# State steps of the second prompt tile inside the joint chunk stage, and one set of weight places for the first tile and the gathers

## The reference, cut to what matters

```python
    def step(S, inp):
        r_t, d_t, k_t, v_t, kk_t, a_t = inp
        Skk = jnp.einsum('bhvk,bhk->bhv', S, kk_t)
        S = (S * d_t[:, :, None, :]
             - Skk[..., None] * (kk_t * a_t)[:, :, None, :]
             + v_t[..., None] * k_t[:, :, None, :])
        y_t = jnp.einsum('bhvk,bhk->bhv', S, r_t)
        return S, y_t
...
    s1, i1 = lax.top_k(s[:, :, 0], PEER_TOPK)
    s2, i2 = lax.top_k(s[:, :, 1], PEER_TOPK)
    cand_s = (s1[..., :, None] + s2[..., None, :]).reshape(n, PEER_HEADS, PEER_TOPK * PEER_TOPK)
...
    top_s, top_pos = lax.top_k(cand_s, PEER_TOPK)
    eidx = jnp.take_along_axis(cand_i, top_pos, axis=-1)
    gate = jax.nn.softmax(top_s, axis=-1)
    u = expert_u[eidx].astype(F32)
    h = jax.nn.gelu(jnp.einsum('nhkd,nd->nhk', u, xr.astype(F32)), approximate=False)
    out = jnp.einsum('nhk,nhkd->nd', gate * h, expert_v[eidx].astype(F32))
```

## Time and profile before

| | us |
|---|---|
| median of 3 runs | 3025.03 |
| lowest, highest | 3024.61, 3034.01 |
| profiled execution | 3024.4 |
| its span | 3022.6 |

### The profile page before, as it was taken

One profiled execution on the slowest core, in us unless ns is written; L12 is line 12 of the kernel. 1 busy time (PEld: TensorE's weight loads), 2 busy tenths in 40 slices (PEclk: granted clock), 3 DMA queues, 4 the chain that ended last, 5 costly groups with the idle time before them and its releaser, 6 DMA issues. The chain is left out here.

```text
span 3022.6 us, 33166 instructions
## 1 busy us (share of the span) xinstructions
PE 2145.5 (71%) x11513; PEld 1128.9 (37%) x11513; DVE 1785.6 (59%) x4171; ACT 683.5 (23%) x1972; POOL 1064.2 (35%) x995
## 2 busy tenths in 40 slices
PE   7989896568776867685577676676857768555554
PEld 3447685325443533332225222243324435222221
DVE  3454438355885754764746847557745455955555
ACT  2222121112222211212511115221113322121111
POOL 1033122333664633333333434333342222354442
PEclk9999898779987978896789787887979879677788
DMA  4330430899989999999999999999999999899998
GB/s 156 104 140 1 163 126 1 307 388 390 409 314 396 387 411 416 373 395 409 358 393 418 404 417 400 358 419 419 388 417 418 419 382 420 306 364 420 420 420 331
DMA packets 152164, 1025.97 MB, mean 339 GB/s; under 512 B 17852, under 2 KB 19180, under 8 KB 34112
## 3 DMA queue, kind: packets, MB, share of 16 engines
q0 software_dynamic: 116416, 823.23, 67.2%
q1 hardware_dynamic: 35584, 200.62, 16.9%
HBM read 1003.34 MB, written 19.44 MB: 338 GB/s over the span
## 5 line engine op out<-in xcount | busy, mean ns | idle before, releaser
L1364 POOL DMA_INDIRECT fl_pairs<-in_peer_uv,fl_row_at x652 | 743.3, 1140 | 1206.4 <-PE fl_acc L1337 1085.4
L1337 PE MATMUL fl_acc<-fl_pairs,fl_diag 128*64 128x512 f32 x2608 | 835.9, 745 | 419.4 <-ACT fl_diag L1310 399.8
L1290 DVE CUSTOM_DVE_ANT_0 fl_pairs<-fl_pairs,fl_rows 128x1024 f32<-128x1024 f32 x652 | 790.2, 1233 | 430.7 <-DMA fl_pairs<-in_peer_uv,fl_row_at 430.0
L1337 PEld LDWEIGHTS fl_acc<-fl_pairs,fl_diag 128*64 128x64 f32 x2608 | 281.0, 161 | 821.2 <-issue 775.2
L1316 ACT ACTIVATE fl_acts<-fl_dots 128x2 f32<-128x2 f32 x384 | 78.1, 203 | 1253.4 <-DVE fl_dots L1290 1253.1
L1310 ACT ACTIVATE fl_diag<-constants_sb,fl_mix 128x64 f32<-128x64 f32 x768 | 224.4, 341 | 292.5 <-DVE fl_mix L1280 291.1
L1337 PE MATMUL fl_acc<-fl_more,fl_diag 128*64 128x512 f32 x464 | 149.5, 743 | 87.2 <-ACT fl_diag L1310 87.1
L1364 POOL DMA_INDIRECT fl_more<-in_peer_uv,fl_row_at x116 | 132.3, 1140 | 219.0 <-PE fl_acc L1337 198.9
L1290 DVE CUSTOM_DVE_ANT_0 fl_more<-fl_more,fl_rows 128x1024 f32<-128x1024 f32 x116 | 139.6, 1222 | 78.5 <-DMA fl_more<-in_peer_uv,fl_row_at 78.1
L1280 DVE TENSOR_TENSOR fl_mix<-fl_row_gate,fl_acts 128x2 f32<-128x2 f32 x384 | 74.7, 195 | 129.0 <-ACT fl_acts L1316 77.4
L1710 PE MATMUL aacc<-pc_piece,at_xT 128*128 128x512 f32 x288 | 138.9, 625 | 8.3 <-PEq L1623 8.3
(11 more groups left out here) (571 smaller groups left out, 2870.6 us busy)
## 6 DMA issues: line engine op xcount, KB each, us to landing
pc_piece<-in_kvq_by_pair SPq DMA_DIRECT2D x36, 1024.0 KB, 9.3
pc_piece<-in_query_by_head SPq DMA_DIRECT2D x32, 1024.0 KB, 9.6
pc_piece<-in_past_k SPq DMA_DIRECT2D x16, 1024.0 KB, 14.1
pc_piece<-in_past_v SPq DMA_DIRECT2D x16, 1024.0 KB, 12.4
ro_w_ring<-in_rwkv_w_rkv SPq DMA_DIRECT2D x24, 512.0 KB, 4.5
pc_piece<-in_out_by_pair SPq DMA_DIRECT2D x12, 1024.0 KB, 9.4
fl_pairs<-in_peer_uv,fl_row_at POOLq DMA_INDIRECT x652, 15.0
ft_ring<-in_query_by_head SPq DMA_DIRECT2D x8, 1024.0 KB, 5.0
```

Of the source, the lines that this page charges most:

```text
L1290: dve.tensor_tensor_reduce(pair, pair, self.rows[:, u % 2, j, :], 1.0, 0.0, ALU.mult, ALU.add, self.dots[:, u % 2, q, j:j + 1]).then_inc(* ...
L1337: mm = pe.matmul(self.acc[j * FOLD:(j + 1) * FOLD, half, :], self.diag[:, self.summed % self.DIAGS, j, :], self.pair(g)[:, D + half * HALF ...
L1364: pool.indirect_dma_start(self.pair(g), None, self.io["peer_uv"], bass.IndirectOffsetOnAxis(ap=self.row_at[:, u % TILES, j, q:q + 1], axis ...
```

## The change

Four parts:

1. In the joint stage a pair's state steps follow its group: one step per tick (PE `state_step`, L2457 of the changed kernel; VectorE `add_state`, L2601), beside the next pair's work; the last pair's eight steps stand at the stage's end. `half_outputs` of tile 1 has no steps left: 6 ticks in place of 13.
2. Four places (`early`) are there from the start. `FirstTile` uses them for its weights, its vectors, its gate and its turned rows; later they are four of the ring's eight places. The rows of tile 0 for the dots have a buffer of their own (`first_rows`), spread at tick 24 in the joint stage.
3. In the joint stage the query weights are used two to a tick (ticks 23 to 30), the choice is drawn together (ticks 27 to 48), the experts' table goes out at tick 52 and comes in at 54, and the first four gathers are issued at tick 55. The gates' table follows on its own.
4. For all six tiles the experts and the gates travel apart: out, in, out, in at four ticks that follow each other, each "in" waiting for its own write. Gathers wait for the experts alone. The turns to end with are 7, 9, 17, 18, 31 in place of 11, 12, 19, 20, 32; from 55 on they are as before.

```diff
@@ Flow @@
-        self.ring, self.rows = sb("pairs", [P, self.KEPT, 2 * D]), sb("rows", [P, 2, GROUPS, D])
+        self.ring, self.rows = sb("pairs", [P, self.KEPT - self.EARLY, 2 * D]), sb("rows", [P, GROUPS, D])
...
-        for u, out_at, in_at in self.turns:
-            if out_at == n:
-                self.turn_rows_out(pool, u)
-            if in_at == n:
-                self.turn_rows_in(pool, u)
+        for u, first in self.turns:
+            if first == n:
+                self.experts_out(pool, u)
+            if first + 1 == n:
+                self.experts_in(pool, u)
+            if first + 2 == n:
+                self.gates_out(pool, u)
+            if first + 3 == n:
+                self.gates_in(pool, u)
...
+    def first_gathers(self, pool):
+
+        pool.wait_ge(*self.expert_in.at(16 * GROUPS))
+        for g in range(self.EARLY):
+            self.gather(pool, g)
@@ half_chunks @@
+                def state_step(g, c):
+
+                    if not prompt or g < 0:
+                        return
+                    if c == 0:
+                        pe.wait_ge(*gp_done.at(g + 1))
+                        pe.wait_ge(*fp_done.at(g + 1))
...
+                    if g + c > 0:
+                        pe.wait_ge(*step_done.at(NCH * g + c))
+                    for r in range(2):
+                        mm = pe.matmul(bank[3][half(r), stepped(c)], x.Ft[half(r), c, g, :], x.G[half(r), c, g, :], tile_position=(r * N, r * N))
+                    mm.then_inc(*step_psum.by())
...
+                    dve.wait_ge(*step_psum.at(NCH * g + c + 1))
+                    dve.tensor_tensor(x.G[:, c + 1, g, :], bank[3][:, stepped(c)], x.G[:, c + 1, g, :], ALU.add).then_inc(*step_done.by())
@@ half_outputs @@
-    TICKS = NCH + 5
+    LEAD = NCH if x.sample else 1
+    TICKS = LEAD + 5
...
+                if not x.sample:
+                    sp.wait_ge(*flow.landed(5))
@@ FirstTile @@
-        if n == self.ticks:
-            self.flow.turn_rows_out(pool, 0)
-            self.flow.turn_rows_in(pool, 0)
+        if n == 24:
+            pool.wait_ge(*self.normed.at(1))
+            self.flow.spread_rows(pool, 0)
+        if n == self.KNOWN + 2:
+            self.flow.experts_out(pool, 0)
+        if n == self.KNOWN + 4:
+            self.flow.experts_in(pool, 0)
+        if n == self.KNOWN + 5:
+            pool.wait_ge(*self.queries.at(4))
+            self.flow.first_gathers(pool)
...
@@ program and experts_and_attention @@
-        half_outputs(core, io, flow, x, rows, 11, rows=((0, 1),))
+        half_outputs(core, io, flow, x, rows, 7)
...
-            second_tile(core, io, flow, x, rows, ops, [(12, {}), (19, {}), (20, {}), (32, {})])
+            second_tile(core, io, flow, x, rows, ops, [(9, {}), (17, {}), (18, {}), (31, {})])
...
-            (110, dict(choose=2, side=15)), (112, dict(side=15)), (125, dict(side=60, end=12, turn=((2, 14, 16),))), (131, {}), (132, {}),
+            (110, dict(choose=2, side=15)), (112, dict(side=15)), (125, dict(side=60, end=12, turn=((2, 13),))), (131, {}), (132, {}),
```

More of the change, by code:

```diff
@@ L2457, in _ @@
                     beside.tensor(pe, tick + 7)
+                    state_step(b - 1, 7)
+                for c in range(NCH):
+                    state_step(NG - 1, c)
             @block.scalar
@@ L2667, in _ @@
                     pe.wait_ge(*start_in.at(16))
-                for c in range(NCH):
-                    if c > 0 and not x.sample:
-                        pe.wait_ge(*step_done.at(c))
-                    elif c > 1:
+                for c in range(NCH if x.sample else 0):
+                    if c > 1:
                         pe.wait_ge(*step_done.at(c - 1))
@@ L2690, in _ @@
                 mm.then_inc(*y_tok.by())
[L2691 removed]
+                for n in range(LEAD + 3, TICKS + 1):
                     flow.tensor(pe, n)
@@ L2695, in _ @@
             def _(act):
-                for n in range(1, NCH + 3):
+                for n in range(1, LEAD + 3):
                     flow.scalar(act, n)
@@ L2709, in _ @@
                 flow.vector(dve, 1)
-                for c in range(NCH):
+                if not x.sample:
+                    flow.vector(dve, 2)
+                for c in range(NCH if x.sample else 0):
                     dve.wait_ge(*step_psum.at(c + 1))
@@ L2902, in vector_steps @@
             part = choice.best_of(dve, choice.scores, q)
-            for i in range(4):
-                advance(part, 6)
-                n += 1
-                if i < 3:
-                    yield n
+            advance(part, 10)
+            yield n + 1
             drain(part)
+            n += 2
         part = choice.rest(dve, 0)
-        while n < self.ticks:
+        while n < self.KNOWN:
             yield n
```

160 lines of the change are left out of this document (105 added, 55 removed).

## The result

| | before | after |
|---|---|---|
| median of 9 runs each, us | 3026.84 | 3043.39 |
| lowest to highest, us | 3024.06 to 3039.56 | 3034.07 to 3057.47 |
| the profiled execution (its span), us | 3024.4 (3022.6) | 3047.2 (3045.4) |

The ratio is 1.0049, with a 95% interval from 1.0034 to 1.0065: the changed kernel is about 15 us slower by the ratio, 16.6 by the medians.

The account below looks back on a forecast made before the run. The prediction took PE and VectorE to bound the start, then idle DMA time to decide. Its terms, +3 (DMA account), -2 (one turn more) and +5 (tables), sum to +6, giving 3030 us; own range 3018 to 3042, whole range 3006 to 3050.

Parts of the forecast that it names:

- Start of the outputs' stage: End of the joint stage: summed tick by tick, the next stage starts at 560 us (bounds 545 and 572), before 538.3.
- the state terms up to there: Joint stage, ticks 1 to 48: state steps add 1.7 at first, 3 on PE, 4.0 on VectorE, 3 for handing over.
- I add 3 for handing over: Joint stage, ticks 31 to 48: PE waits for VectorE in each tick with a state step, 3 us in all.
- GpSimd's wait for the gate table: End of the joint stage: the sum to 560 has no term of its own for this wait.
- The signs of the mechanism: Joint stage: VectorE above 90% busy from 457 to 520, PE waiting for `step_done`; DMA share near 0.9 for 50 us after.
- The DMA account: Behind the outputs' stage's start: the same bytes are through at 638 against 635, +3 us, with 9 us of holes.
- One turn more in the stage to 55: Stage to turn 55, 24 turns for 23: part of the added turn fills DMA holes, -2 us (bounds -5 and 0).
- The tables' way: Tables of tiles 2 and 3: two waits each, no gather behind the write, +5 us (bounds 0 and 20).
- Taking the state steps out of `half_outputs` gives nothing by itself: Outputs' stage of tile 1: 541 to 590 us was full of gathers, which covered the steps; gain 0.
- Free state steps: Faster rival, joint stage: steps fit in gaps, next stage starts at 545 to 548, 3011 us; chance 0.33.
- The double wait: Slower rival, tables of tiles 1 to 3: two waits empty the DMA queue, 23 us in place of 5, 3048; chance 0.22.
- Early gathers late: Rival, end of the joint stage: GpSimd reaches tick 55 late, four gathers start with the next stage, 3040; chance 0.07.

Follow-up runs that it names:

- e7: e5 with all state steps in the outputs' stage, as in the kernel before; 3001.05 us, ratio 0.9903.
- e5: The changed kernel with one wait for both tables of tiles 1 to 5, and tile 0's gate table awaited three ticks later; 3019.11 us, ratio 0.9971.
- e9: The changed kernel, but for tiles 2 and 3 each write and its wait stand two ticks apart, with gathers between; 3027.67 us, ratio 1.0005.
- e4: The changed kernel without the four gathers ahead of the joint stage's end; 3046.36 us, ratio 1.0058.
- e6: e5 with the state steps of pairs 4 to 7 moved to the outputs' stage; 3003.25 us, ratio 0.9914.

## Why the prediction was right or wrong

The forecast was 3030, 6 us over before. Measured were 3043.4, about 15 over: outside the forecast's own 3018 to 3042 and 5 under the slower rival's 3048. The whole range, 3006 to 3050, held it, but it was made wide enough for the faster and the slower rival both, so that says little. By the prediction's own signs the start of the outputs' stage was near enough (6.6 us from 560, with 10 allowed), and the windows behind the tables were not: they lost 12.5, and more than 12 was to say that the forecast is wrong.

- **What bounds the kernel.** Right: idle DMA time decides. The ruler's pieces (10.1, 3.8, 13.3 and -4.5) add up to the 22.7 us of the trace, and the two large ones are idle DMA time.
- **Start of the outputs' stage: 560, was 566.6.** Up to the choice's table the sum held: the table was ready at 517.9 for 519.6. That was in part luck: the state terms up to there (1.7, 3, 4 and 3, 11.7 in all) were too large, since e7 without steps has its table at 510.3, only 7.6 to 9.8 us ahead of the changed kernel and e5, and the terms of the other work were too small by 2.4. What failed is the step behind it: the sum starts ticks 49 to 63 where VectorE ends the choice, and PE was not there yet. An in-order PE carries its products behind a wait (7.67 us for one add), so the copy of pair 5, at the end of tick 48, came 5.8 us behind the table; in e7 it came 4.9 ahead of it. "I add 3 for handing over" has this at 3; on PE's path, from copy to copy, the steps cost 11 there (e5 less e7). From the table to the outputs' stage it took 48.7 us where 40.4 were summed, 43.7 in e5, where the wait for the gates stands later, and 28.6 in e7.
- **GpSimd's wait for the gate table: nothing, was 3.1.** This is the second term of the start that failed. The wait was priced for GpSimd and not for what stands behind it on that queue, `K_by_chunk`, for which PE waits 3.1 us.
- **The other terms of the start** were near: 6.8 for the last pair's eight steps, measured 558.94 to 566.2 (7.3), or 6.5 by e5 less e7; 0.22 for an add, measured 0.20 to 0.23 (the prediction's estimate of 0.19 was low). Less near was the beginning: up to pair 3's copy the steps cost 9.8, where the terms 1.7 and 3 gave 4.7 to a place some ticks ahead of it. The signs of the mechanism came: VectorE was busy 57.4 of the 63 us from 457 to 520 (91%), PE waited 23.9 us for state adds from 430 to 560, and the DMA share in the 50 us from 567 was 0.88.
- **The DMA account: +3, was +7.9.** Its working held: between 567 and 652 the engines moved 85 x 0.375 = 31.9 MB, 76.8 us' worth at 0.415, so 8.2 us were lost where I wrote 9. From the program's start to 652 us they moved 92.93 MB before and 89.67 after (the lists of DMA issues for 0 to 652 us); the 3.3 MB between them are 7.9 us. The stage's start, 6.6 late, accounts for the excess over 3; the first gather, 0.6 us behind the start where 2 were counted, and the 0.8 of the holes take back 2.2: 3 + 6.6 - 2.2 = 7.4.
- **One turn more in the stage to 55: -2.** Not seen: between gathers 32 and 92, and 92 and 236, the traces scatter by more.
- **The tables' way: 5, was 13.3** for tiles 2 and 3 (13.6 to 17.5 against the seven kernels with gathers behind the write). This is the step that failed most, and by its own row: I leaned on the share of 0.99 from 1360 to 1365 as if it were the covered case, though two gathers had been issued behind that write and none would be now. The bounds, 0 to 20, and the rival's mechanism (no gather behind the write) were right, e9 shows it; its price of 5 us for each of four waits was too high on the whole: the idle shares of the 5 us windows add up to 8.4 us behind tile 2's two waits (1365 to 1390), 5.9 of them behind the first, and 4.1 behind tile 3's (1785 to 1810), 12.5 in all. Tiles 4 and 5, which keep two gathers, cost next to nothing: the shares behind tile 4's tables stay at 1.00 to 1.02, and behind tile 5's one window is at 0.91.
- **"Taking the state steps out of `half_outputs` gives nothing by itself."** Right as far as the runs can tell: e7 does them there, under the gathers, and is 18 us faster than e5.
- **The rivals.** Free state steps: no, they cost 25 us of the joint stage. The double wait: yes for its mechanism, as said above, but its 3048 came near also because the stage's start, which it had at 560, was late. Early gathers late: no, the first came at 532.7 as the text wanted; but they brought next to nothing in the changed kernel, since the gates' write stood behind them (e4).

## What to carry to other kernels

Work that hands over between two in-order engines belongs where neither is full, and where other work covers the whole chain: the 64 state steps cost nothing that the runs can tell under the gathers (e7 against e6) and 25 us in the stage that the gathers wait for. When a write is read back through HBM, queue transfers behind it before the engine that issues them waits. Count what is behind it, not how long the wait is: a wait of 21.6 us with two gathers behind the write cost nothing (e9), and waits of 28.2 and 8.9 us with none behind left the DMA engines idle for 8.4 us. And price a wait by what stands behind it on its queue.

## What was not expected of the hardware

A write of one table behind four gathers of 1 MB took 9.6 us from its issue to its fetch, and 3.5 us with none ahead (9.3 and 3.1 from issue to landing): here a small transfer's end was set by the big ones before it. PE idled up to 7.7 us at a time for adds of 0.21 us, and its granted clock fell: it was 1.00 from 500 to 507.8, 0.51 during the wait of 7.67 us and still 0.50 behind it, from 515.4 to 523.7, while PE was busy 7.7 of 8.3 us. Windows (columns as in rows 2) of before, where it stayed at 1.00, and of after, the stretches between the copies of G of pairs 3, 4 and 5:

```profile
472.00:487.20 15.20, 12.74 (x139) 10.47 (x139) 12.97 (x48) 3.73 (x10) 4.30 (x5) 1.00 0.01 2
487.20:504.00 16.80, 13.14 (x139) 10.60 (x140) 16.37 (x69) 3.79 (x11) 6.35 (x8) 1.00 0.01 1
```
```profile
470.50:493.10 22.60, 16.68 (x171) 13.24 (x172) 20.75 (x71) 3.69 (x11) 7.43 (x6) 0.92 0.00 1
493.10:523.70 30.60, 18.38 (x171) 14.35 (x171) 24.42 (x50) 3.74 (x11) 5.33 (x6) 0.74 0.00 1
```

Behind the wait, PE's own matmuls are slower; the same four in the kernel after, at a granted clock of 0.50 (1.2 GHz, 518 to 523) and later at 1.00 (2.4 GHz, 538 to 541):

```profile
520.39 0.48 PE L2441 MATMUL hc_bank_1w<-hc_x_1w,hc_B_by_chunk_1w 128*64 128x64 f32 x4
...
538.42 0.34 PE L2441 MATMUL hc_bank_1w<-hc_x_1w,hc_B_by_chunk_1w 128*64 128x64 f32 x4
```

So part of a wait's price is paid again behind it. That part was not measured apart.
